# Expert rows of a mixture-of-experts stage: gather and store by bounds, results stored by token

## The chip, the cores and the metric

The kernel runs on one core of a Trainium2 chip. The core has five engines with instruction streams of their own: TensorE (PE; its weight loads are listed apart as PEld), VectorE (DVE), ScalarE (ACT), GpSimd (POOL) and SyncE (SP), which here only issues DMAs. Sixteen DMA engines move data between HBM and the on-chip memory. The metric is the device time of one execution in microseconds; lower is better. Engines wait for each other through semaphores; a DMA raises its semaphore by 16 in all.

## The reference

One layer of a decoder for 1,024 prompt tokens and 64 sample tokens: a forgetting attention and a chunked gating MLP run side by side and are merged, then a mixture of experts, then a gated embedding and the last norm. The change touches the mixture of experts and what reads its result. Everything is float32.

```
def hier_moe(h, w_rg, b_rg, w_re, b_re, w_g, w_u, w_d):     # h: 1088 x 1024
    glog = h @ w_rg + b_rg                                   # 4 groups
    gsel = argmax(glog); pg = softmax(glog)[gsel]
    elog = (h @ w_re + b_re)[group gsel]                     # 8 experts in it
    topv, topi = top_k(softmax(elog), 2); topv /= sum(topv)
    expert_idx = gsel * 8 + topi;  wts = pg * topv
    ...
    yb = (silu(xb @ w_g[e]) * (xb @ w_u[e])) @ w_d[e]        # 1024 -> 512 -> 1024, for each expert's tokens
    out = sum over a token's two experts of wts * yb
...
x2 = x + hier_moe(rmsnorm(x))
x3 = x2 + sigmoid(rmsnorm(x2) @ w_ple_gate + b) * rmsnorm(p @ w_ple_proj)
y  = rmsnorm(x3)
```

So 1,088 tokens make 2,176 rows of expert work, spread over 32 experts. The three weight matrices of an expert are 2 MiB each. With the inputs of the reference the experts get, in order of size, 113, 103, 96, 94, 87, 85, 84, 84, 83, 81, 80, 76, 76, 75, 75, 64, 64, 60, 60, 59, 59, 56, 54, 54, 54, 53, 47, 43, 43, 41, 39 and 34 rows.

## The kernel before, in words

The program is a row of stages, each a block in which all five engines run their own lists; engines meet in a barrier at the end of a block. The last ones are `stage_route` (its engine lists run at the head of the block of `stage_moe`), `stage_moe`, `stage_overflow`, `stage_final`.

**Units.** The rows are laid into 22 units of 128 slots (`NUNIT`), which is 2,816 slots. Experts are ranked by their number of rows. The first 5 fill a unit alone ("full"), from slot 0 up. The next 14 have slots 0 to 95 of a unit, and slots 96 to 127 of two such units together hold one of 7 smaller experts, 32 rows each ("split"). The last 6 share three units, slots 0 to 63 and 64 to 127 ("half"). Within each of these stretches the rows stand at its low end and the empty slots at its high end. Rows over an expert's room would go to up to 25 spare units (`NOVER`), which `stage_overflow` computes in a loop that runs only if there are any; with these inputs there are none.

**Routing.** DVE ranks the experts and computes each row's slot. PE turns this into a list of tokens by slot (`c.bank[2]`, 47 columns of 128 slots, line 2432); an empty slot comes out as token 0. DVE copies the list to `c.idx_i` (lines 2593 and 2594, `c.idx_done`), POOL waits for it, and then DVE works out which expert has which rank (`perm_i`, to line 2602), for which the weight loads from the sixth on wait (`perm_done`).

**The expert loop.** For each unit u: POOL gathers 128 rows of 4 KiB from `moe_in` with one indirect DMA (`gather_rows`, line 2295), PE transposes them (2682), multiplies by gate and up weights (2688), transposes the product (2713) and multiplies by down weights (2727); DVE and ACT keep the intermediate results, ACT copies the unit's result out of PSUM (2763, `keep_y`) and stores it to `moe_out` as a plain block of 128 rows (2765) from its own DMA queue. There are two buffers for gathered rows and two for results. PE's order is fixed: gate(u+1) first half, turn(u), gate(u+1) second half, down(u), transposes(u+2), up(u+1). SP issues the 96 weight loads of 2 MiB in the order in which they are used into a ring of 7 slots (line 2242); each waits until PE is done with what the slot held. Where a unit has four stretches PE runs the four 32-row pieces beside each other.

**The final stage.** For each of 9 tiles of tokens, POOL gathers the two result rows of every token from `moe_out` with two indirect DMAs (2983), by `c.slot_i`; DVE adds them with their weights (3063, 3066); PE, ACT, DVE and POOL do the rest, and SP stores the result. POOL waits first for all stores of results (`c.y_out`).

**Spare rows.** `moe_out` has 47 x 128 rows. While an earlier stage (`stage_mlp` and its neighbours) runs, POOL writes zeros over the 25 x 128 spare rows with five DMAs (line 1083).

Of the kernel before, what the change touches and what calls it, by code (L numbers as in the profile page):

```python
# [21 lines left out]
P = 128  # L22
D = 1024
# [939 lines left out]
def stage_prompt_attention(nc, c):  # L963
# [12 lines left out]
    zeros = view(c, T_AT + 64, D // 2)  # L976
# [10 lines left out]
    blank, c.blank_out = c.sem("blank"), c.kept_sem("blank_out")  # L987
# [26 lines left out]
    with nc.Block() as block:  # L1014
        @block.sync
        def _(sp):
# [47 lines left out]
            sp.wait_ge(c.blank_out, 16 * BLANKS)  # L1064

        @block.gpsimd
        def _(pool):
            pool.wait_ge(c.out_rows, 16 * 5)
            g_ = nc.gpsimd
            g_.memset(zeros, 0.0).then_inc(blank, 1)  # L1070
# [214 lines left out]
BLANKS = 5  # L1285
# [867 lines left out]
SLOTS = (NUNIT + NOVER) * P  # L2153
# [95 lines left out]
def stage_route(nc, c):  # L2249
# [3 lines left out]
    def take(*dims):  # L2253
        v = view(c, at[0], *dims)
        at[0] += int(np.prod(dims))
        return v
# [17 lines left out]
    lane, block_at, tok = take(P), take(NB), take(NT)  # L2274
# [35 lines left out]
    c.idx_i = view(c, T_AT + 3200, NB).bitcast(I32)  # L2310
    c.idx = view(c, T_AT + 40, NB)
    c.over_i = view(c, T_AT + 88, NOVER + 1).bitcast(I32)
    assert NB <= 48 and NOVER < 28
# [33 lines left out]
    def route_pool(pool):  # L2347
# [13 lines left out]
        g.iota(tok, pattern=[[P, NT]], base=0, channel_multiplier=1,  # L2361
# [6 lines left out]
        g.memset(tok[NS:P, NP:NT], 0.0).then_inc(aux, 1)  # L2368
        pool.wait_ge(aux, 10)
        g.memset(PR[NS:P, NPR, :], 0.0).then_inc(aux, 1)  # L2370

# [97 lines left out]
    def route_dve(dve):  # L2469
# [113 lines left out]
        for r in range(2):  # L2583
            tt(ON_BLOCK[:, r], over_tiles(block_at, NB), bcast(hi[:, r], NB), ALU.is_equal)
            tt(ON_BLOCK[:, r], ON_BLOCK[:, r], bcast(tok, NB), ALU.mult)
# [7 lines left out]
        v.tensor_copy(c.idx_i, c.bank[2][:, 0:NB]).then_inc(c.idx_done, 1)  # L2593
        v.tensor_copy(c.idx, c.bank[2][:, 0:NB]).then_inc(c.idx_done, 1)
# [19 lines left out]
def stage_moe(nc, c):  # L2614
# [17 lines left out]
    with nc.Block() as block:  # L2632
# [115 lines left out]
        def _(act):  # L2748
# [9 lines left out]
            def keep_y(u):  # L2758
                b = UNITS[u][0]
# [4 lines left out]
                act.wait_ge(y_done, u + 1)  # L2764
                act.dma_start(c.y_d[b * P:(b + 1) * P, :], Y[:, u % 2, :]).then_inc(y_out[u % 2], 16)
# [44 lines left out]
def stage_overflow(nc, c):  # L2810
# [8 lines left out]
    idx = view(c, T_AT + 116, 1).bitcast(I32)  # L2819
# [13 lines left out]
    with nc.Block() as block:  # L2833
        @block.sync
        def _(sp):
            n = blocks(sp)
            with sp.Fori(0, NOVER // GROUP) as group:
                with sp.If(group * GROUP < n):
                    with sp.Fori(0, GROUP) as j:
                        i = group * GROUP + j  # L2840
                        e = sp.value_load(c.over_i[0:1, bass.ds(i, 1)], min_val=0, max_val=NE - 1)
                        row = i * P + NUNIT * P
# [3 lines left out]
                        sp.wait_ge(y_done, i + 1)  # L2846
                        sp.dma_start(c.y_d[bass.ds(row, P), :], Y).then_inc(stored, 16)
# [4 lines left out]
        def _(pool):  # L2852
            n = blocks(pool)
            with pool.Fori(0, NOVER // GROUP) as group:
                with pool.If(group * GROUP < n):
                    with pool.Fori(0, GROUP) as j:
                        i = group * GROUP + j
                        pool.wait_ge(picked, i + 1)
                        pool.sem_inc(step_end, 1)
                        nc.gpsimd.indirect_dma_start(out=XG, out_offset=None, in_=c.h2_d,  # L2860
                                                     in_offset=bass.IndirectOffsetOnAxis(ap=idx, axis=0)
                                                     ).then_inc(x_in, 16)
# [45 lines left out]
        def _(dve):  # L2908
            v = nc.vector
            n = blocks(dve)  # L2910
            with dve.Fori(0, NOVER // GROUP) as group:
                with dve.If(group * GROUP < n):
                    with dve.Fori(0, GROUP) as j:
                        i = group * GROUP + j
                        v.tensor_scalar(idx, c.idx[:, bass.ds(i + NUNIT, 1)], 1.0, None, ALU.mult).then_inc(picked, 1)
# [8 lines left out]
                                        ALU.mult).then_inc(act_kept, 1)  # L2924

# [7 lines left out]
def stage_final(nc, c):  # L2933
# [22 lines left out]
    with nc.Block() as block:  # L2956
# [194 lines left out]
def finish(nc, c):  # L3151

    with nc.Block() as block:
        @block.sync
        def _(sp):
# [5 lines left out]
            sp.wait_ge(c.blank_out, 16 * BLANKS)  # L3161
# [88 lines left out]
```

## Time and profile before

| what | value |
|---|---|
| median of 3 runs | 1824.93 us (1823.78 to 1824.99) |
| the profiled execution's own time | 1823.42 us |
| its span, first to last instruction | 1821.8 us |
| its mean granted PE clock | 0.969 of full speed |
| expert loop, from the first gate product to the end of the last down product | 1141.27 to about 1660.6 us |
| final stage, first DMA issue to the end of the span | 1668.24 to 1821.8 us |
| bytes read from and written to HBM | 360.50 MB, 52.37 MB |

The profile is of one execution; times are in microseconds from the span's start. In a timeline a row has its start, its length, the engine, the line of the kernel, the operation, what it writes and reads, how many instructions were merged into the row, and in brackets how long the engine had stood idle before it and what ended that. "issue" in brackets is time for which the profile shows no releaser. The DMA share is the mean busy share of the 16 DMA engines.

### The profile page before, as it was taken

The page shows a single profiled execution, that of the slowest core. Times are in us where ns is not written, and L with a number is a line of the kernel's source. Part 1 is how long each engine was busy: PE and PEld are TensorE (multiplying, and loading weights), DVE is VectorE, ACT ScalarE, POOL GpSimd, SP SyncE. Part 2 cuts the span into 40 slices and gives each one's busy share as a digit, 9 for nine tenths or more (in the row PEclk, how much of TensorE's full clock was granted, in tenths as well). Part 3 has the DMA queues.
Part 4 walks back from the last instruction along what each step waited for, and adds up shares of the span by engine and source line. Part 5 has one row for each costly group of instructions (what it writes and reads, how often), then busy time and mean ns, then how long its engine had stood idle before and what let it go on. Part 6 is the DMA issues. An engine that isn't in the chain of part 4 may idle for free. (4 is left out here: it accounts for less than half of the span.)

```text
span 1821.8 us, 27384 instructions
## 1 busy us (share of the span) xinstructions
PE 1692.8 (93%) x10679; PEld 932.2 (51%) x10679; DVE 631.2 (35%) x1233; ACT 309.3 (17%) x565; POOL 291.2 (16%) x375
## 2 busy tenths in 40 slices
PE   7999999998999988988799979999989999995997
PEld 4588888645777753544564435433333334332443
DVE  4622111145555665655134346111001011111565
ACT  2010100012333333321200114100000000000222
POOL 2202212042000021332105410100000000001230
PEclk9999999998999988998899998999999999997999
DMA  6031223202535449998711155999999999998341
GB/s 202 3 86 54 76 68 124 89 0 82 200 107 176 153 146 355 368 383 287 299 48 71 76 221 224 342 404 428 427 426 428 427 427 427 410 426 310 115 150 59
DMA packets 130835, 414.68 MB, mean 228 GB/s; under 512 B 31033, under 2 KB 61306, under 8 KB 118418
## 3 DMA queue, kind: packets, MB, share of 16 engines
q1 hardware_dynamic: 94674, 312.79, 44.8%
q0 software_dynamic: 19488, 68.21, 10.2%
q10 hardware_dynamic: 16544, 31.93, 4.6%
q8 instruction: 86, 1.41, 0.3%
q14 instruction: 43, 0.35, 0.1%
HBM read 360.50 MB, written 52.37 MB: 227 GB/s over the span
## 5 line engine op out<-in xcount | busy, mean ns | idle before, releaser
L2688 PE MATMUL psum<-arena 128*32 128x512 f32 (+2 forms) x2144 | 312.5, 594 | 5.3 <-issue 3.9
L440 PE MATMUL psum<-arena 128*128 128x272 f32 x1120 | 259.5, 393 | 0.0
L440 PEld LDWEIGHTS psum<-arena 128*128 128x128 f32 x1120 | 211.6, 190 | 43.7 <-issue 0.9
L2688 PEld LDWEIGHTS psum<-arena 128*32 128x32 f32 (+2 forms) x2144 | 98.2, 118 | 186.6 <-issue 182.1
L2727 PE MATMUL psum<-arena 128*32 128x512 f32 (+2 forms) x1072 | 159.0, 604 | 13.3 <-issue 11.5
L1146 PE MATMUL psum<-arena 128*128 128x272 f32 x512 | 131.2, 400 | 1.2 <-ACT arena L1174 1.2
L3047 PE MATMUL psum<-arena 128*128 128x512 f32 x256 | 113.7, 602 | 1.4 <-DVE arena L3073 1.4
L2727 PEld LDWEIGHTS psum<-arena 128*32 128x32 f32 (+2 forms) x1072 | 53.4, 120 | 116.1 <-issue 116.1
L2782 DVE TENSOR_TENSOR arena<-psum,g_moe_rows 128x1024 f32<-128x1024 f32 x22 | 26.9, 1224 | 245.8 <-PE psum L2682 245.8
L1974 PE MATMUL psum<-arena 128*128 128x512 f32 x224 | 102.1, 607 | 3.3 <-PEq L1749 1.6
L1146 PEld LDWEIGHTS psum<-arena 128*128 128x128 f32 x512 | 93.6, 193 | 17.0 <-ACT arena L1174 1.3
L2295 POOL DMA_INDIRECT arena<-moe_in,arena x22 | 21.6, 982 | 453.6 <-PE psum L2682 413.2
L3047 PEld LDWEIGHTS psum<-arena 128*128 128x128 f32 x256 | 48.8, 194 | 60.1 <-issue 60.1
L1417 POOL DMA_DIRECT2D arena<-in_cache_v x112 | 60.1, 537 | 117.3 <-PE psum L1521 110.2
L1452 PE MATMUL psum<-arena 128*128 128x512 f32 x160 | 73.4, 601 | 2.6 <-DVE arena L1649 2.6
L1635 DVE STREAM_TRANSPOSE arena<-arena 128x2048 f32<-128x2048 f32 x28 | 63.9, 2297 | 18.7 <-DMA arena<-in_cache_k 18.6
L1974 PEld LDWEIGHTS psum<-arena 128*128 128x128 f32 x224 | 41.7, 193 | 52.3 <-issue 52.3
L2756 ACT ACTIVATE arena<-psum 128x512 f32<-128x512 f32 x22 | 13.1, 597 | 318.6 <-PE psum L2688 318.6
L1181 ACT ACTIVATE arena<-arena 128x128 f32<-128x128 f32 (+7 forms) x64 | 49.1, 768 | 103.6 <-DVE arena L1239 63.2
L2790 DVE TENSOR_TENSOR arena<-arena,psum 128x512 f32<-128x512 f32 x22 | 15.1, 687 | 141.2 <-PE psum L2688 141.2
L887 PE MATMUL psum<-arena 128*128 128x512 f32 x128 | 56.8, 598 | 4.1 <-PEq L132 3.3
L429 PE MATMUL psum<-arena 128*128 128x512 f32 x128 | 56.8, 597 | 0.0
(334 smaller groups left out, 1910.4 us busy)
## 6 DMA issues: line engine op xcount, KB each, us to landing
arena<-in_w_exp_gate SPq DMA_DIRECT2D x32, 2048.0 KB, 17.9
arena<-in_w_exp_up SPq DMA_DIRECT2D x32, 2048.0 KB, 18.5
arena<-in_w_exp_down SPq DMA_DIRECT2D x32, 2048.0 KB, 17.1
arena<-in_cache_v POOLq DMA_DIRECT2D x128, 256.0 KB, 9.3
arena<-in_cache_k SPq DMA_DIRECT2D x124, 256.0 KB, 7.9
arena<-in_w_in SPq DMA_DIRECT2D x18, 1024.0 KB, 6.0
moe_out<-arena POOLq DMA_DIRECT2D x5, 2560.0 KB, 11.1
moe_out<-arena ACTq DMA_DIRECT2D x22, 512.0 KB, 11.4
```

The lines of the kernel that those rows point to most:

```text
L429: last = mm(c.bank[4 + t % 3][:, :], hidden_tile(c, k, t), WV[:, k, :], start=(k == 0), stop=(k == KD - 1))
L440: last = mm(bank[:, s, :], w[:, k, :], x[:, k, SUB * s:SUB * s + SUB], start=start and k == 0, stop=(k == KD // 2 - 1), skip_group_check=True)
L887: last = mm(c.bank[t % 2][:, :], hidden_tile(c, k, t), W[:, k, :], start=(k == 0), stop=(k == KD - 1))
L1146: done = mm(c.bank[7][:, 0:SUB], WG[blk % 2][:, k, q * P:(q + 1) * P], hidden_part(c, k, th, s), start=(k == 0), stop=(k == KD - 1))
L1181: s.activation(S[:, m % 2, hl, 0:w], S[:, m % 2, hl, 0:w], ACT.Exp, bias=low[:, m % 2, hl:hl + 1], scale=-1.0, accum_out=total[:, m % 4, h ...
L1417: pool.dma_start(VC[:, ch, g, :], c.cache_v[bass.ds(numbers[ch][g] * P, P), :]).then_inc(v_in[ch], 16)
L1452: last = mm(c.bank[7][:, :], UP[col % 2][:, n, k, :], src[:, 4 * half:4 * half + 4, k, :], start=(k == 0), stop=(k == KF - 1))
L1635: v.transpose(keys, keys).then_inc(turned[b % 2], 1)
L1974: last = mm(bank, x[:, k, :], w[:, k, :], start=start and k == 0, stop=k == KD // 2 - 1, skip_group_check=True)
L2688: last = mm(out[rows_, :], XT[:, u % 2, k, rows_], c.ring_tile(LOAD[kind, r])[:, k, :], start=(k == 0), stop=(k == KD - 1))
L2727: last = mm(y_ps[rows_, cols], ACT_T[:, k, rows_], c.ring_tile(LOAD["down", r])[:, k, cols], start=(k == 0), stop=(k == KF - 1))
L3047: last = mm(gate_ps[t % 2][:, half * 512:half * 512 + 512], XT[:, t % 2, k, :], c.wpg[half][:, k, :], start=(k == 0), stop=(k == KD - 1))
```

## The change

Empty slots no longer stand for token 0: token numbers are counted from 1, so that an empty slot comes out as 0, and DVE turns the list into two: `c.idx_i`, the row of `moe_in` to gather (first or second expert of the token alike), and `c.dest_i`, the row of `moe_out` to write (the token's number, plus 2,048 for its second expert). Empty slots get an index from 8,191 up in both. Gathers and stores of results are indirect DMAs with `bounds_check` and `oob_is_err=False`, so rows with such an index are left out. The gathered buffer is cleared once on POOL. The stores move from ACT's list to POOL's, as a scatter by token. `moe_out` has 3,136 rows, the first experts' results by token from row 0 and the second experts' from row 2,048, so that the final stage reads plain blocks. The zeros over the spare rows, and the waits for them, are gone. The overflow loop is changed in the same way.

```
-            pool.wait_ge(blank, 1)
-            spare = c.y_d[NUNIT * P:].rearrange("(p n) (a d) -> p (n a) d", p=P, a=2)
-            each = 2 * NOVER // BLANKS
-            for q in range(BLANKS):
-                pool.wait_ge(gate_mm, 5 * q + 4)
-                pool.dma_start(spare[:, q * each:(q + 1) * each, :],
-                               zeros.unsqueeze(1).to_broadcast([P, each, D // 2])).then_inc(c.blank_out, 16)
...
-                             in_offset=bass.IndirectOffsetOnAxis(ap=c.idx_i[:, b:b + 1], axis=0)
-                             ).then_inc(xg_in[u % 2], 16)
+                             in_offset=bass.IndirectOffsetOnAxis(ap=c.idx_i[:, b:b + 1], axis=0),
+                             bounds_check=SEQ + NS - 1, oob_is_err=False).then_inc(xg_in[u % 2], 16)
...
-        g.iota(tok, pattern=[[P, NT]], base=0, channel_multiplier=1,
+        g.iota(tok, pattern=[[SECOND, 2], [P, NT]], base=1, channel_multiplier=1,
...
+        pool.wait_ge(aux, 11)
+        g.memset(XG, 0.0).then_inc(aux, 1)
+        pool.wait_ge(aux, 12)
...
-        v.tensor_copy(c.idx_i, c.bank[2][:, 0:NB]).then_inc(c.idx_done, 1)
-        v.tensor_copy(c.idx, c.bank[2][:, 0:NB]).then_inc(c.idx_done, 1)
+        found = c.bank[2][:, 0:NB]
+        do(v.tensor_scalar(empty, found, 0.5, float(NOWHERE), ALU.is_lt, ALU.mult))
+        do(v.tensor_scalar(other, found, SECOND + 0.5, -float(SECOND), ALU.is_ge, ALU.mult))
+        do(v.scalar_tensor_tensor(out=place_of, in0=found, scalar=-1.0, in1=empty, op0=ALU.add, op1=ALU.add))
+        tt(row_of, place_of, other, ALU.add)
+        v.tensor_copy(c.idx_i, row_of[:, 0:NUNIT]).then_inc(c.idx_done, 1)
+        v.tensor_copy(c.dest_i, place_of[:, 0:NUNIT]).then_inc(c.idx_done, 1)
+        v.tensor_copy(c.idx, row_of[:, NUNIT:]).then_inc(c.idx_done, 1)
+        v.tensor_copy(c.dest, place_of[:, NUNIT:]).then_inc(c.idx_done, 1)
...
-            for u in range(2, NUNIT):
-                pool.wait_ge(xt_tr, u - 1)
-                c.gather_rows(g, u)
+            def gather(u):
+                if u < NUNIT:
+                    pool.wait_ge(xt_tr, u - 1)
+                    c.gather_rows(g, u)
+            def scatter(u):
+                b = UNITS[u][0]
+                pool.wait_ge(y_done, u + 1)
+                g.indirect_dma_start(out=c.y_d, out_offset=bass.IndirectOffsetOnAxis(ap=c.dest_i[:, b:b + 1], axis=0),
+                                     in_=Y[:, u % 2, :], in_offset=None, bounds_check=Y_ROWS - 1, oob_is_err=False
+                                     ).then_inc(y_out[u % 2], 16)
+            gather(2)
+            gather(3)
+            for u in range(NUNIT):
+                scatter(u)
+                gather(u + 4)
...
-                act.wait_ge(y_done, u + 1)
-                act.dma_start(c.y_d[b * P:(b + 1) * P, :], Y[:, u % 2, :]).then_inc(y_out[u % 2], 16)
...
+                n = P if t < NP else NS
                 for r in range(2):
-                    g.indirect_dma_start(out=YG[:, t % 2, r, :], out_offset=None, in_=c.y_d,
-                                         in_offset=bass.IndirectOffsetOnAxis(ap=c.slot_i[:, r, t:t + 1], axis=0)
-                                         ).then_inc(yg_in[t % 2], 16)
+                    at = SECOND * r + t * P
+                    pool.dma_start(YG[0:n, t % 2, r, :], c.y_d[at:at + n, :]).then_inc(yg_in[t % 2], 16)
```

On DVE, at the end of the routing, before the change (2593 and 2594 copy the list for POOL; the two after them begin the ranks for `perm_i`):

```order
L2590 TENSOR_TENSOR arena<-arena 128x384 x6
L2593 CAST arena<-psum 128x47
L2594 COPY arena<-psum 128x47
L2483 TENSOR_TENSOR arena<-arena 1x1024 x2
L2601 TENSOR_REDUCE arena<-arena 1x32
L2602 CAST arena<-arena 1x32
```

and with it:

```order
L2585 TENSOR_TENSOR arena<-arena 128x384 x6
L2589 TENSOR_SCALAR arena<-psum 128x47
L2590 TENSOR_SCALAR arena<-psum 128x47
L2591 SCALAR_TENSOR_TENSOR arena<-psum,arena 128x47
L2478 TENSOR_TENSOR arena<-arena 128x47
L2593 CAST arena<-arena 128x22
L2594 CAST arena<-arena 128x22
L2595 COPY arena<-arena 128x25
L2596 COPY arena<-arena 128x25
L2478 TENSOR_TENSOR arena<-arena 1x1024 x2
L2603 TENSOR_REDUCE arena<-arena 1x32
L2604 CAST arena<-arena 1x32
```

Four operations stand ahead of the first copy, and six instructions more ahead of the ranks.

On POOL, from the routing's last memset to the end of the expert block, before:

```order
L2370 MEMSET arena 64x256
L2295 DMA arena<-moe_in,arena 128x1024 x2
L2378 TENSOR_SCALAR arena<-arena 128x9
L2380 TENSOR_TENSOR arena<-arena,neghalf 128x9
L2295 DMA arena<-moe_in,arena 128x1024 x20
L2632 UNCONDITIONAL_BRANCH
```

and the last of it with the change (2286 is the gather now, 2667 the scatter of results, 2634 the end of the block, 2845 the first read of the overflow block):

```order
L2286 DMA arena<-moe_in,arena 128x1024
L2667 DMA moe_out<-arena 3136x1024
L2286 DMA arena<-moe_in,arena 128x1024
L2667 DMA moe_out<-arena 3136x1024
L2286 DMA arena<-moe_in,arena 128x1024
L2667 DMA moe_out<-arena 3136x1024 x4
L2634 UNCONDITIONAL_BRANCH
L2862 UNCONDITIONAL_BRANCH
L2845 TENSOR_LOAD arena
```

The 22 stores now alternate with the gathers on POOL, and the last four, which wait for ACT's last copies, are the last thing that POOL does in the block.

## Rows read from the trace of the kernel before

**Rows 1.** The page: busy time of each engine, share of the span, instructions.

```profile
PE 1692.8 (93%) x10679; PEld 932.2 (51%) x10679; DVE 631.2 (35%) x1233; ACT 309.3 (17%) x565; POOL 291.2 (16%) x375
```

**Rows 2.** Five stretches: length; busy of PE, PEld, DVE, ACT, POOL; clock, DMA, GB/s.

```profile
1141.27:1276.80 135.53, 135.53 (x840) 51.47 (x840) 15.61 (x18) 9.79 (x12) 8.62 (x9) 1.00 0.96 391
1276.80:1480.00 203.20, 187.81 (x1430) 67.40 (x1432) 20.82 (x24) 13.57 (x17) 7.50 (x8) 0.99 1.01 427
1480.00:1640.00 160.00, 160.00 (x1128) 59.11 (x1124) 18.21 (x21) 11.34 (x14) 4.68 (x5) 1.00 1.00 422
1640.00:1661.00 21.00, 18.04 (x84) 6.17 (x76) 1.38 (x2) 1.35 (x2) 0.00 (x0) 0.92 1.02 407
440.00:620.00 180.00, 179.86 (x1244) 132.31 (x1244) 98.70 (x392) 64.70 (x160) 7.12 (x13) 1.00 0.46 159
```

**Rows 3.** Timeline of PE: start, length, operation, count, [idle before it <-releaser].

```profile
1131.93 7.03 PE L2406 MATMUL psum<-arena 128*128 128x512 f32 x16
1138.80 1.06 PE L2682 MATMUL psum<-ident,arena 128*128 128x128 f32 x8
...
1278.91 7.07 PE L2727 MATMUL psum<-arena 128*32 128x512 f32 x64 [2.11 <-issue]
```

**Rows 4.** The same, later in the expert loop.

```profile
1435.94 1.16 PE L2682 MATMUL psum<-ident,arena 128*128 128x128 f32 x8
...
1458.58 1.16 PE L2682 MATMUL psum<-ident,arena 128*128 128x128 f32 x8
...
1476.32 7.07 PE L2727 MATMUL psum<-arena 128*32 128x512 f32 x64 [1.90 <-issue]
...
1651.85 8.78 PE L2727 MATMUL psum<-arena 128*64 128x512 f32 x32 [1.80 <-DMA arena<-in_w_exp_down]
```

**Rows 5.** DMA from 1340 to 1480 us: queues, then issues with us to landing.

```profile
q1 hardware_dynamic: 3700, 53.94, 90.5%
q0 software_dynamic: 804, 2.90, 5.1%
q10 hardware_dynamic: 785, 2.82, 5.0%
...
moe_out<-arena ACTq DMA_DIRECT2D x5, 512.0 KB, 12.1
arena<-moe_in,arena POOLq DMA_INDIRECT x5, 12.5
```

**Rows 6.** Timeline of DVE: two small chained operations late in the routing.

```profile
1116.46 0.18 DVE L2579 CAST arena<-arena 128x18 int32<-128x18 f32 x1
1116.67 0.18 DVE L2580 TENSOR_SCALAR arena<-arena 128x18 int32<-128x18 int32 x1
```

**Rows 7.** Timeline of POOL: the routing stage's last memset, the first gather.

```profile
1086.55 0.31 POOL L2370 MEMSET arena<- 64x256 f32 x1
1126.78 1.77 POOL L2295 DMA_INDIRECT arena<-moe_in,arena  x1 [39.92 <-DVE arena L2594]
```

**Rows 8.** Timeline of all engines, from the last unit into the final stage.

```profile
1660.67 1.02 ACT L2763 ACTIVATE arena<-psum 128x1024 f32<-128x1024 f32 x1 [18.09 <-PE psum L2727]
1661.72 0.34 ACTq L2765 DMA_DIRECT2D moe_out<-arena  x1
1668.24 0.81 SPq L2961 DMA_DIRECT2D arena<-ple_rows  x2
1669.00 0.94 POOL L2983 DMA_INDIRECT arena<-moe_out,arena  x1 [93.43 <-POOLq L2833]
1670.24 0.94 POOL L2983 DMA_INDIRECT arena<-moe_out,arena  x1 [0.30 <-issue]
...
1676.26 1.28 DVE L3063 SCALAR_TENSOR_TENSOR arena<-arena 128x1024 f32<-128x1024 f32 x1 [25.48 <-DMA arena<-moe_out,arena]
```

**Rows 9.** The page: a group of plain DMAs issued on POOL.

```profile
L1417 POOL DMA_DIRECT2D arena<-in_cache_v x112 | 60.1, 537 | 117.3 <-PE psum L1521 110.2
```

**Rows 10.** DMA issues from 1655 to 1680 us: count, KB each, us to landing.

```profile
moe_out<-arena ACTq DMA_DIRECT2D x1, 512.0 KB, 6.0
```

More of the change, by code:

```diff
@@ L975, in stage_prompt_attention @@
     pace = view(c, T_AT + 24, 16)
-    zeros = view(c, T_AT + 64, D // 2)
     NRAW = 4
@@ L1063, in _ @@
             c.load_keys(sp, 1, 2)
-            sp.wait_ge(c.blank_out, 16 * BLANKS)
         @block.gpsimd
@@ L1069, in _ @@
             g_ = nc.gpsimd
-            g_.memset(zeros, 0.0).then_inc(blank, 1)
             g_.memset(c.CN, 0.0).then_inc(c.cleared, 1)
@@ L1282, in _ @@
                     keep_out(m - 2)
-BLANKS = 5
 CH = 4
@@ L2152 @@
 NOVER = 25
-SLOTS = (NUNIT + NOVER) * P
+SECOND = 2048
+NOWHERE = 8192
+Y_ROWS = SECOND + SEQ + NS
 def unit_plan():
@@ L2273, in stage_route @@
     pick = GT.rearrange("p a b -> p (a b)")[:, 0:NOVER * NE].rearrange("p (s e) -> p s e", e=NE)
-    lane, block_at, tok = take(P), take(NB), take(NT)
+    lane, block_at, tok = take(P), take(NB), take(2, NT)
+    empty, other, place_of, row_of = [take(NB) for _ in range(4)]
     slot_f, lo, hi = take(2, NT), take(2, NT), take(2, NT)
@@ L2309, in stage_route @@
     c.slot_i = view(c, T_AT + 20, 2, NT).bitcast(I32)
-    c.idx_i = view(c, T_AT + 3200, NB).bitcast(I32)
-    c.idx = view(c, T_AT + 40, NB)
+    c.idx_i = view(c, T_AT + 3200, NUNIT).bitcast(I32)
+    c.dest_i = view(c, T_AT + 3200 + NUNIT, NUNIT).bitcast(I32)
+    c.idx, c.dest = view(c, T_AT + 38, NOVER), view(c, T_AT + 38 + NOVER, NOVER)
     c.over_i = view(c, T_AT + 88, NOVER + 1).bitcast(I32)
-    assert NB <= 48 and NOVER < 28
+    assert 2 * NUNIT <= 50 and 2 * NOVER <= 50
     step, aux = c.sem("route_step"), c.sem("route_aux")
@@ L2367, in route_pool @@
         pool.wait_ge(aux, 9)
-        g.memset(tok[NS:P, NP:NT], 0.0).then_inc(aux, 1)
+        g.memset(tok[NS:P, :, NP:NT], 0.0).then_inc(aux, 1)
         pool.wait_ge(aux, 10)
         g.memset(PR[NS:P, NPR, :], 0.0).then_inc(aux, 1)
+        pool.wait_ge(aux, 11)
+        g.memset(XG, 0.0).then_inc(aux, 1)
+        pool.wait_ge(aux, 12)
         pool.wait_ge(c.idx_done, 2)
@@ L2584, in route_dve @@
             tt(ON_BLOCK[:, r], over_tiles(block_at, NB), bcast(hi[:, r], NB), ALU.is_equal)
-            tt(ON_BLOCK[:, r], ON_BLOCK[:, r], bcast(tok, NB), ALU.mult)
+            tt(ON_BLOCK[:, r], ON_BLOCK[:, r], bcast(tok[:, r], NB), ALU.mult)
         for ch in range(NCHUNK):
@@ L2758, in keep_y @@
             def keep_y(u):
-                b = UNITS[u][0]
                 act.wait_ge(down_mm, u + 1)
@@ L2818, in stage_overflow @@
     ACT_T, Y = view(c, MOE_AT + 5 * D, KF, P), view(c, MOE_AT + 6 * D, D)
-    idx = view(c, T_AT + 116, 1).bitcast(I32)
+    idx, dest = view(c, T_AT + 116, 1).bitcast(I32), view(c, T_AT + 117, 1).bitcast(I32)
     gate_ps, up_ps, turn_ps, y_ps, x_ps = c.bank[0], c.bank[1], c.bank[2], c.psum_pair(2), c.psum_pair(3)
@@ L2841, in _ @@
                         e = sp.value_load(c.over_i[0:1, bass.ds(i, 1)], min_val=0, max_val=NE - 1)
-                        row = i * P + NUNIT * P
                         for w, src, n_rows in ((wg, c.w_gate, D), (wu, c.w_up, D), (wd, c.w_down, FF)):
@@ L2845, in _ @@
                                          ).then_inc(w_in, 16)
-                        sp.wait_ge(y_done, i + 1)
-                        sp.dma_start(c.y_d[bass.ds(row, P), :], Y).then_inc(stored, 16)
                         sp.wait_ge(stored, i * 16 + 16)
@@ L2857, in _ @@
                         i = group * GROUP + j
-                        pool.wait_ge(picked, i + 1)
+                        pool.wait_ge(picked, i * 2 + 2)
                         pool.sem_inc(step_end, 1)
                         nc.gpsimd.indirect_dma_start(out=XG, out_offset=None, in_=c.h2_d,
-                                                     in_offset=bass.IndirectOffsetOnAxis(ap=idx, axis=0)
-                                                     ).then_inc(x_in, 16)
+                                                     in_offset=bass.IndirectOffsetOnAxis(ap=idx, axis=0),
+                                                     bounds_check=SEQ + NS - 1, oob_is_err=False).then_inc(x_in, 16)
+                        pool.wait_ge(y_done, i + 1)
+                        pool.sem_inc(step_end, 1)
+                        nc.gpsimd.indirect_dma_start(out=c.y_d, out_offset=bass.IndirectOffsetOnAxis(ap=dest, axis=0),
+                                                     in_=Y, in_offset=None, bounds_check=Y_ROWS - 1, oob_is_err=False
+                                                     ).then_inc(stored, 16)
         @block.tensor
@@ L2914, in _ @@
                         i = group * GROUP + j
-                        v.tensor_scalar(idx, c.idx[:, bass.ds(i + NUNIT, 1)], 1.0, None, ALU.mult).then_inc(picked, 1)
+                        v.tensor_scalar(idx, c.idx[:, bass.ds(i, 1)], 1.0, None, ALU.mult).then_inc(picked, 1)
+                        v.tensor_scalar(dest, c.dest[:, bass.ds(i, 1)], 1.0, None, ALU.mult).then_inc(picked, 1)
                         dve.wait_ge(x_tr, i + 1)
@@ L2924, in _ @@
                                         ALU.mult).then_inc(act_kept, 1)
+                        dve.wait_ge(stored, i * 16 + 16)
 def final_weights(c):
@@ L3160, in _ @@
             sp.wait_ge(c.consts_in, 16 * 7)
-            sp.wait_ge(c.blank_out, 16 * BLANKS)
             for sem in c.h2_out:
@@ L3245 @@
     c.e_d = nc.dram_tensor("ple_rows", (SEQ + NS, D), F32).ap()
-    c.y_d = nc.dram_tensor("moe_out", (SLOTS, D), F32).ap()
+    c.y_d = nc.dram_tensor("moe_out", (Y_ROWS, D), F32).ap()
     program(nc, c)
```

1 line of the change is left out of this document (removed).

## The prediction, made before the changed kernel ran

> **What bounds the kernel now.** The page's busy line comes first: TensorE is busy for 1692.8 of 1821.8 us [rows 1], so other engines matter only where PE waits or where the DMA engines are full. A table by stretches then splits the part that the change touches [rows 2]. From 1141 to 1277 us PE does not pause and the DMA share climbs to 0.96. From 1276.8 to 1480 the DMA engines are at 1.01 with 427 GB/s and PE is busy for 187.81 of 203.20: it stands still for 15.39 us. From 1480 to 1640 it does not pause. PE's timeline shows what the idle time looks like: pauses of 2 to 3 us ahead of a product, the first of 2.11 us at 1276.8 and the last of 1.90 us before 1476.32 [rows 3, 4]. The profile names no releaser ("issue"), but each stands ahead of a product whose weights must have landed, inside a stretch with full DMA engines; the one before 1651.85 (1.80 us) is named, a down weight [rows 4]. I read them all as late weights. A unit without a pause takes PE 22.64 us (1435.94 to 1458.58 [rows 4]).
>
> So the loop is within a few per cent of two limits. The weights are 32 x 3 x 2.097 = 201 MB; gathers and stores add 22 x 2 x 0.524 = 23 MB. In the full stretch the weights have 90.5% of the engines' time, POOL's queue with the gathers 5.1%, ACT's queue with the stores 5.0% [rows 5]. Behind the loop, the timeline shows the last result copied at 1661.69, stored from ACT at 1661.72, the next block entered at 1668.24 and the first final gather at 1669.00 [rows 8]. From 1677 on PE runs the final stage nearly alone.
>
> **The change part by part.**
>
> *Zeros over spare rows.* They ran between 455 and 620 us. There PE is busy for 179.86 of 180 us and the DMA engines are at 0.46 [rows 2]. Nobody waited; removing them gives at most the 0.14 us. I take 0.
>
> *Routing.* DVE has four more operations ahead of the first copy. Chained operations of this size start 0.21 us apart (1116.46, 1116.67 [rows 6]): 0.84 us, so the first gather goes from 1126.78 [rows 7] to 1127.6. PE is in the embedding's products until it takes up the gathered rows at 1138.80 without a pause [rows 3]; if the gather lands as the store at a quiet moment did, in 6.0 us [rows 10], it is there at 1133.6, 5 us early; with the 12.5 us of the full loop [rows 5] at 1140.1, which would cost at most the 0.84 that it starts later. The ranks, and the sixth weight load behind them, come 0.84 + 2 x 0.12 = 1.1 us later. The loads after it wait for slots that PE frees, so the delay is not carried on. I take 0, bounds 0 and +1.1. Clearing the gather buffer on POOL is 128x2048 against 64x256 in 0.31 us [rows 7]: at most 2.5 us, in 40 us in which POOL waits [rows 7]. Cost 0.
>
> *Empty slots.* 2,816 - 2,176 = 640 slots are empty, 22.7%. Each gather and each store shrinks by 0.119 MB on average, 0.28 us at 427 GB/s. What this is worth is decided by how the bytes are spread over the 16 DMA engines. A weight has landed only when all 16 have added their part (the code waits for multiples of 16). If the saving is spread evenly, all are ahead by 0.28 us per transfer. If each engine serves fixed slots it is not: the empty slots stand at the high end of their stretches. With the counts of the reference's inputs slots 0 to 42 are full in every unit, slots 0 to 58 in all but the three shared by halves; 596 of the 640 empties lie in slots 59 to 127. Engines that serve the low slots then move what they moved before, and PE waits for them. No row shows which engine serves a slot; the bounds come from PE's pauses. Below: nothing saved, 0. Above: nine units lie between the first and the last pause of the full stretch, 9 x 2 x 0.28 = 5.0 us of traffic, plus the first pause of 2.11, which what was saved earlier covers: 7.1 us; and the 1.80 before 1651.85: 8.9 in all. The row nearest to the question is the full stretch at 1.01: no engine has spare time to give to another, so a saving counts only on the engine that has it. The empties lie on the high slots, so I take the lower end, 0, for this part.
>
> The Trainium skill ("DMA: Bandwidth & Descriptors", The descriptor swizzle) gives such a fixed assignment for a 128-partition transfer from GpSimd: eight engines serve partitions 0 to 63, eight 64 to 127, in groups of four. By it the engine with partitions 0 to 3 and 32 to 35 would have no empty slot in any unit, and the sum stays at 0; whether an indirect transfer with left-out rows follows it no row here shows.
>
> *One queue fewer.* Stores and gathers were in flight together, 12.1 and 12.5 us each [rows 5], on two queues beside the weights. On POOL's one queue they go one behind the other, and both have 45 us (two units) until needed, so part of this traffic moves behind weights that PE waits for. In a backlog such a shift counts once, not per unit: at most one transfer, 0.524 MB at 427 GB/s = 1.2 us. I take -1.2, bounds -1.2 and 0. On POOL the scatter waits for ACT's copy, and behind it is queued the gather for four units on; it comes about 1 us later and is needed 45 us later. ACT loses 0.34 us per unit [rows 8], in idle time.
>
> *End of the block.* The last store was 0.34 us on ACT after the copy; as an indirect DMA it is 0.94 us on POOL (the final gathers' length [rows 8]) plus about 0.1 us for the wait. POOL reaches the barrier at 1661.69 + 1.04 = 1662.7 instead of ACT at 1662.06: +0.7. The store's landing took 6.0 us [rows 10], to 1667.7, before the first final gather at 1669.00; a scatter that starts moving 0.7 us later lands at 1668.4, and the gather is then due at 1669.7. Covered by 1.3 us. I take +0.7, bounds +0.4 and +5.3 (below, C).
>
> *Final reads.* The first two gathers are issued 1.24 us apart [rows 8]. A plain DMA on POOL takes 0.54 us [rows 9], with the same 0.3 between: 0.84. The second read is 0.4 us earlier; part is lost since the rows come at the engines' rate. I take -0.3, bounds -0.8 and +0.5. The later ones lie beside PE.
>
> Sum: 0 + 0 + 0 - 1.2 + 0.7 - 0.3 = -0.8 us. The profiled execution took 1823.42 us, 1.6 over its span and 1.5 under the median of 1824.93; with the change it would take 1822.6, and the median comes to 1824.1. By the bounds without C and without an even saving, -2.0 to +2.3: 1822.5 to 1827. About 0.2% (3.7 us) is what a measurement of this kernel can tell from no change; "same" is 1821.3 to 1828.6.
>
> **The rivals.**
>
> *A, the forecast:* the engines with the low slots keep their traffic. 1824.1.
>
> *B, the saving is even over the engines* (left-out rows are packed away before rows are dealt out, or slots are dealt out in turn). For it: 22.7% less in both kinds of transfer, and PE's 15.39 us of pauses under a DMA share of 1.01. Against it: the empties' place. Up to -8.9 with the tail's +0.4: 1816.4; dealt out in turn (slot modulo 16) the engine with the fewest empties has 26 where the mean is 40, two thirds of it, so -5.9 + 0.4: 1819.4. Chance 27%.
>
> *C, the last scatter lands late.* The slower side. In the loop a gather from POOL takes 12.5 us to land beside the weights [rows 5], and the last scatter meets the 4 MB of final-stage weights that SP issued just before. The final reads wait for it. If it takes 12.5 us from 1661.8, they start at 1674.3 instead of 1669.0, +5.3, and nothing is behind which to hide it; it decides from a landing of 7.9 us on. Against it: the plain store there landed in 6.0 [rows 10]. 1824.9 + 5.3 - 1.2 - 0.3 = 1828.7, more where the scatter's rows, spread over HBM, take longer. Chance 12%.
>
> The Trainium skill ("DMA: Bandwidth & Descriptors", Latency and other measured facts) gives the first byte as about 1 us for DMAs from GpSimd and 0.6 for those from SP and ACT; by it the last landing would be 0.4 later, inside the cover.
>
> *D, the change doesn't do what it says:* a left-out row costs its engine as much as a moved one. The loop keeps its time apart from the queue: also 1824.1, or with nothing from the queue 1825.3. Chance 8%.
>
> **How the numbers follow.** A 53%, B 27%, C 12%, D 8%. Likeliest: 1824.1, its own range 1822.5 to 1827. B lies below 1821.3 with nearly all of its weight, and A with a little: faster 28%. C, at 1828.7 or more, gives slower with two thirds of its weight, and the unknown costs in A and D add 4%: 12%. Same 60%. The range from 1817.0 to 1828.4 leaves out half of C and the far half of B.
>
> **What would show it.** Right: in the changed profile PE's idle time in the stretch from 1277 to 1480 is still 12 us or more, while the bytes of POOL's queue in the loop are about 23% under those of the two queues before; the first final read starts 0.5 to 1 us later after ACT's last copy; PE's work up to 1141 is at the same times within 1 us. Wrong: the pauses shrink to half or less (B); the final reads are released by the scatter's landing (C); POOL's queue moves as many bytes as the two before (D).

## The result and the profile after the change

The changed kernel took 1825.82 us (median of 20 runs, 1818.86 to 1830.17) where the kernel before took 1822.78 us beside it (20 runs, 1818.99 to 1827.71). The ratio is 1.0017, 95% interval 1.0010 to 1.0025: 3 us slower. The forecast was 1824.1 against 1824.93, no change that can be measured. The time lies inside its range; the side is that of rival C, and what was forecast for the parts is far from what was measured, as shown below.

The page's busy line of the changed kernel, its windows (columns as in [rows 2]):

```profile
PE 1695.7 (93%) x10679; PEld 933.2 (51%) x10679; DVE 631.2 (35%) x1239; ACT 309.3 (17%) x565; POOL 304.0 (17%) x392
```

```profile
1141.27:1276.80 135.53, 135.20 (x840) 51.20 (x838) 15.63 (x18) 9.72 (x13) 13.98 (x13) 1.00 0.96 392
1276.80:1480.00 203.20, 191.85 (x1452) 69.53 (x1456) 20.83 (x24) 13.32 (x17) 16.23 (x16) 0.98 1.00 423
1480.00:1640.00 160.00, 160.00 (x1126) 58.92 (x1119) 18.23 (x21) 12.24 (x15) 12.16 (x12) 1.00 0.99 413
...
440.00:620.00 180.00, 179.86 (x1243) 132.63 (x1243) 98.80 (x392) 65.44 (x162) 2.27 (x8) 1.00 0.28 89
```

The zeros over spare rows are gone (159 to 89 GB/s in the last row) and PE is busy for the same 179.86 us. In the full stretch PE stands still for 11.35 us where it was 15.39 [rows 2].

The DMA queues from 1160 to 1640 us, first of the kernel before (packets, MB, share), then of the changed one:

```profile
DMA packets 17903, 201.02 MB, mean 419 GB/s; under 512 B 1983, under 2 KB 1983, under 8 KB 6847
...
q10 hardware_dynamic: 2880, 10.49, 5.4%
q0 software_dynamic: 2592, 9.44, 4.8%
```

```profile
DMA packets 18015, 198.28 MB, mean 413 GB/s; under 512 B 3062, under 2 KB 3062, under 8 KB 6860
...
q0 software_dynamic: 5472, 15.56, 8.1%
```

POOL's one queue moves 22% less than the two did (15.56 against 19.93 MB). The packets under 512 B rose by 1079, and the 4.37 MB that are missing are 1067 rows of 4096 bytes: in the records a left-out row is a packet of 4 bytes and 9 ns where a moved row has 4096 bytes and 159 ns.

The timeline of the changed kernel from the last unit into the final stage, to be held against [rows 8]:

```profile
1655.71 1.02 ACT L2779 ACTIVATE arena<-psum 128x1024 f32<-128x1024 f32 x1 [15.57 <-PE psum L2744]
1657.51 0.98 POOL L2667 DMA_INDIRECT moe_out<-arena  x1 [15.62 <-ACT arena L2779]
1670.58 0.82 SPq L2979 DMA_DIRECT2D arena<-ple_rows  x2
1671.12 2.19 POOL L3003 DMA_DIRECT2D arena<-moe_out  x4 [12.64 <-POOLq L2847]
1677.90 1.28 DVE L3081 SCALAR_TENSOR_TENSOR arena<-arena 128x1024 f32<-128x1024 f32 x1 [29.57 <-DMA arena<-moe_out]
```

The last copy starts 4.96 us earlier than before and the first final read 2.12 us later. The span is 1.9 us longer, and this divides into four pieces, between the first gate product, the last copy, the first read and the first sum on DVE:

| piece | after, us | before, us | difference |
|---|---|---|---|
| start of the loop | 1140.93 | 1141.27 | -0.34 |
| loop | 514.78 | 519.40 | -4.62 |
| copy to first read | 15.41 | 8.33 | +7.08 |
| read to sum | 6.78 | 7.26 | -0.48 |

Together they are +1.64; the rest comes later.

What stands in the 15.41 us is seen only when one asks for the line that ends the block (events of the engines' sequencers: count, ns, start). The changed kernel:

```profile
L2634 POOLq EVENT_SEMAPHORE  x2: 17/17/17, 1665.1 to 1665.2; - x2
L2634 DVEq DRAIN  x1: 725/725/725, 1647.7 to 1647.7; - x1
L2634 SPq DRAIN  x1: 123/123/123, 1647.8 to 1647.8; - x1
...
L2634 ACTq DRAIN  x1: 1052/1052/1052, 1655.7 to 1655.7; - x1
L2634 POOLq DRAIN  x1: 7469/7469/7469, 1657.3 to 1657.3; - x1
```

And the kernel before, the same line of it:

```profile
L2632 POOLq EVENT_SEMAPHORE  x2: 17/17/17, 1662.3 to 1662.4; - x2
L2632 POOLq DRAIN  x1: 14061/14061/14061, 1574.4 to 1574.4; - x1
...
L2632 SPq DRAIN  x1: 123/123/123, 1651.8 to 1651.8; - x1
...
L2632 ACTq DRAIN  x1: 157/157/157, 1662.1 to 1662.1; - x1
```

At a block's end each engine drains, then all meet. In the kernel before SP and ACT drain in 0.12 and 0.16 us although their DMAs are in flight: ACT had issued a store 0.4 us before, which landed at 1667.7. ACT's 1.05 us in the changed kernel lie beside its last copy; no DMA of its own is in flight then. POOL's drain is another thing: 7.47 us here, 14.06 us before, where it began behind the last gather and lay beside the loop. Before, the last gather landed at 1587.5 and the drain ended at 1588.5. In the changed kernel the last scatter was issued at 1657.51 and took 5.4 us to land, to 1662.9; the drain ends at 1664.8, 1.9 us later, and the engines meet at 1665.2. Before they met at 1662.4, 0.7 us after the copy's end; now it is 8.5 us. Behind it the overflow block takes its 5.2 us (1665.3 to 1670.5; before 5.8, 1662.4 to 1668.2), which used to cover the store's landing and now stands in series with it. There POOL's drain, with nothing of its own in flight, takes 0.05 to 0.06 us in both kernels, so the 7.47 us are not what a drain on POOL always costs. The row of 14.06 us was there to be read before.

### The profile page after: what moved, and what is told of

It is laid out like the page before. It is cut to its first block and busy times, and to the rows that moved or that the text cites. A ratio compares the mean times of both kernels' runs of the same rounds, so it can differ in the third digit from the quotient of the medians.

```text
span 1823.7 us, 27423 instructions
## 1 busy us (share of the span) xinstructions
PE 1695.7 (93%) x10679; PEld 933.2 (51%) x10679; DVE 631.2 (35%) x1239; ACT 309.3 (17%) x565; POOL 304.0 (17%) x392
## 5 line engine op out<-in xcount | busy, mean ns | idle before, releaser
L2667 POOL DMA_INDIRECT moe_out<-arena x22 | 22.2, 1008 | 461.7 <-PE psum L2699 280.2
```

## The experiments

Each ratio is to the kernel before, run beside it. "Loop" is, here and below, the time from the start of the loop's first gate product to the start of its last copy, in the profiled execution. The start itself moves between 1138 and 1147 us from one profile to another, so spans alone compare badly. Two profiles of one and the same kernel gave loops of 515.14 and 516.51, of another 518.96 and 518.94. The loop of the kernel before was 519.40, and 517.59 in the run below that changes its last store alone. A difference between two loops of under 2 us is therefore not read as one.

**Is it POOL's drain?** The first kernel is the changed one with the last unit's scatter issued from the overflow block:

```
-            for u in range(NUNIT):          # expert block, POOL
+            for u in range(NUNIT - 1):
...
+            nc.gpsimd.indirect_dma_start(out=c.y_d, ...)   # overflow block, POOL, first
```

> The changed kernel, with the last unit's scatter issued at the head of the overflow block instead of at the end of the expert block. Drain theory (at the end of a block POOL's drain waits until its last DMA has landed; in the changed kernel it lasts 7.47 us and holds all engines at the barrier): POOL's drain in the expert block is short, the landing hides behind the 5 us of the overflow block's own instructions, and the first final read comes 4.5 to 6 us sooner after the last copy than in the changed kernel, so the time is 0.9970 to 0.9990 of the kernel before. Rival (the scatter's issue and landing are themselves what the final stage waits for): the same delay only moves into the next block; ratio 1.001 to 1.003.

1819.72 us, ratio 0.9978 (0.9968 to 0.9988). Its timeline and its drains:

```profile
1657.19 1.02 ACT L2779 ACTIVATE arena<-psum 128x1024 f32<-128x1024 f32 x1 [15.58 <-PE psum L2744]
1659.53 0.97 POOL L2864 DMA_INDIRECT moe_out<-arena  x1 [16.17 <-issue]
1665.10 0.82 SPq L2983 DMA_DIRECT2D arena<-ple_rows  x2
1665.63 2.19 POOL L3007 DMA_DIRECT2D arena<-moe_out  x4 [5.12 <-POOLq L2847]
```

```profile
L2634 POOLq EVENT_SEMAPHORE  x2: 17/17/17, 1658.3 to 1658.4; - x2
L2634 POOLq DRAIN  x1: 10172/10172/10172, 1642.2 to 1642.2; - x1
...
L2634 ACTq DRAIN  x1: 1052/1052/1052, 1657.2 to 1657.2; - x1
```

The drain of the expert block is not short, as expected, but 10.17 us, and hidden beside the last unit; the scatter's landing lies beside the overflow block. From copy to first read it is 8.44 us, against 8.33 before the change. Against the changed kernel the ratio falls by 0.39%, 7.1 us: as much as the +7.08.

The landing is not hidden in full. In the overflow block POOL drains again, now with the scatter in flight:

```profile
L2847 POOLq DRAIN  x1: 2662/2662/2662, 1662.2 to 1662.2; - x1
L2847 PEldq DRAIN  x1: 13/13/13, 1663.6 to 1663.6; - x1
```

The scatter landed at 1664.76 and this drain ended at 1664.85, 1.3 us after PE, the last of the others, was ready.

The other way round, the kernel before with its last plain store moved from ACT to POOL, with the waits for it, and nothing else:

```
+            pool.wait_ge(y_done, NUNIT)
+            pool.dma_start(c.y_d[b * P:(b + 1) * P, :], Y[:, (NUNIT - 1) % 2, :]).then_inc(c.y_last, 16)
...
+                if u == NUNIT - 1:              # ACT: no store of the last unit
+                    return
```

> The kernel before, with the last unit's store alone, still a plain block of 128 rows, issued from POOL instead of ACT. Drain theory: POOL's drain lasts until the store has landed, 5 to 8 us, and the first final read comes 4 to 8 us later after the last copy: ratio 1.002 to 1.0045. Rival (it is the indirect form or the scattered rows that cost): under 1 us, ratio 1.000 to 1.0005.

1830.35 us, ratio 1.0036 (1.0024 to 1.0049).

```profile
1663.04 1.02 ACT L2767 ACTIVATE arena<-psum 128x1024 f32<-128x1024 f32 x1 [16.30 <-PE psum L2731]
1664.36 0.59 POOL L2662 DMA_DIRECT2D moe_out<-arena  x1 [84.64 <-ACT arena L2767]
1677.24 0.81 SPq L2967 DMA_DIRECT2D arena<-ple_rows  x2
```

```profile
L2633 POOLq DRAIN  x1: 7448/7448/7448, 1664.3 to 1664.3; - x1
```

The store landed at 1670.79, the drain ended at 1671.78, and the first read came 14.98 us after the copy, 6.65 later than before. So the cost needs neither the indirect form nor left-out rows: one 512 KB store issued from POOL as the last thing of a block costs 7.4 us of drain and makes this kernel 0.36% slower.

**Are the left-out rows worth something in the loop?** The changed kernel with nothing left out (an empty slot gathers row 0 and is stored to a spare row of its own), and the kernel before with bounds on its gathers alone, stores plain on ACT:

> The changed kernel with nothing left out: empty slots gather row 0 again and are stored to spare rows of their own, so that the bytes are those of before and only the queue (gathers and scatters both on POOL) is new. If the queue shortened the pauses: PE idle in 1277 to 1480 stays near 11 us and the ratio is near that of the changed kernel, 1.001 to 1.0025. If the bytes did it: PE idle back at 15 us, ratio 1.003 to 1.005, since the drain stays.

> The kernel before, with only the gathers leaving out empty slots (and the list prepared for it); stores stay plain blocks on ACT. Theory that the bytes left out shorten PE's pauses: half of the bytes, so about half of the 4 us by which the pauses between 1277 and 1480 us shrank, no longer block end: ratio 0.9980 to 0.9995. Rival (one DMA queue fewer is what shortened the pauses): pauses as before, 15 us, ratio 0.9995 to 1.0005.

Full rows: 1830.14 us, 1.0031 (1.0018 to 1.0045), loop 518.98. Short gathers on the kernel before: 1820.87 us, 0.9986 (0.9975 to 0.9998), loop 516.22. By the loops 4.2 us hang on the rows of the changed kernel (518.98 against 514.78) and 3.2 on the gathers' of the kernel before (519.40 against 516.22), by the ratios 2.6 in both pairs, where the forecast had 0. The next three test its reason, the fixed slots: they are the kernel with the late scatter, and their gathers leave out more slots of every unit, full ones too. The edit is a column `far` with 8192 on the named slots, added to the gathers' rows:

```
+        do(v.memset(far, 0.0))
+        do(v.memset(far[64:128], 8192.0))
...
         tt(row_of, place_of, other, ALU.add)
+        tt(row_of, row_of, far, ALU.add)
```

> The kernel with the late last scatter, in which the 22 gathers leave out slots 64 to 127 as well (835 more rows, 3.42 MB; the rows computed for them are stale, scatters as before). 1819.72 us and 13.61 us of pauses between 1276.8 and 1480 are the base. Theory A (each DMA engine serves fixed slots, four by four, eight engines the low 64 and eight the high 64): the engines with the fullest slots still move 176 rows each, nothing is saved, pauses stay at 12 to 15 us and the time at 1819.7 within 1.5. Theory B (what is left is spread evenly): nine units of the stretch save 1.40 MB, 3.3 us at 427 GB/s: pauses near 10, time near 1816. By A eight of the sixteen parts of a gather's landing come several us ahead of the others, by B all come together.

> As the kernel without the high 64 slots, but the gathers leave out slots 32 to 63 and 96 to 127 (1068 more rows than the late last scatter, 4.37 MB). Theory A: every one of the sixteen engines has half of its slots left out, the fullest goes from 176 rows to 88: over nine units 2.36 MB at the whole rate, 5.5 us; pauses near 8, time near 1814. Theory B: 4.37 of 22 units are 1.79 MB in nine, 4.2 us; pauses near 9.5, time near 1815.5. So by A this kernel is 4 to 6 us faster than the one without the high 64 slots, by B within 1 us of it.

> As the two others, but the gathers leave out slots 0 to 63 (1341 more rows, 5.49 MB). Theory A: the eight engines of the high slots still move up to 146 rows where the fullest engine moved 176, 17% less: at most 1.9 us over nine units; pauses near 12, time 1818 to 1819.5. Theory B: 2.25 MB in nine units, 5.3 us; pauses near 8.5, time near 1814.5.

Without the high 64: 1821.43 us, 0.9987 (0.9975 to 0.9998), loop 517.26. Without the low 64: 1819.24 us, 0.9982 (0.9973 to 0.9991), loop 516.29. Without 32 to 63 and 96 to 127: 1812.85 us, 0.9944 (0.9931 to 0.9956), loop 509.41. The windows of the full stretch, of the late scatter and then of the three in that order:

```profile
1276.80:1480.00 203.20, 189.59 (x1444) 69.27 (x1440) 20.82 (x24) 13.56 (x17) 16.20 (x16) 0.99 1.01 423
```

```profile
1276.80:1480.00 203.20, 190.90 (x1429) 68.68 (x1425) 20.84 (x24) 13.56 (x17) 16.20 (x16) 0.98 1.00 416
```

```profile
1276.80:1480.00 203.20, 188.76 (x1436) 68.76 (x1432) 20.84 (x24) 13.57 (x17) 16.19 (x16) 0.99 0.99 412
```

```profile
1276.80:1480.00 203.20, 195.73 (x1496) 69.77 (x1492) 22.06 (x25) 14.60 (x18) 17.04 (x17) 0.98 1.01 424
```

The low 64 are the most rows (1341 against 1068) and gain nothing; the spread ones gain 0.34% and take PE's idle time from 13.61 to 7.47 us. Bytes saved on one set of eight engines are worth nothing, on both sets they are worth about what they weigh. An even spread (B) is refuted: it expected 3.3 and 5.3 us from the high and the low 64.

**But then why do the empties count?** They leave the engines of the lowest slots what they had. Four kernels look at this: full rows with the late scatter, so without the drain's cost, then the same with a row of its own for each empty slot instead of row 0, then that with the high and with the low half of the gathers left out:

> The kernel with the late last scatter, with every slot gathered and stored (empty ones read row 0 and go to spare rows of their own). It isolates what the left-out rows are worth, free of GpSimd's drain at the end of the block. 640 rows in each direction, 5.24 MB; nine units of the full stretch have 2.14 MB of it, 5.0 us. Theory A (fixed slots): the same as with the rows left out, 1819.7 within 1.5. Theory B (even): 4 to 9 us slower, 1824 to 1828. A third (the changed kernel against the one with full rows gave 1825.8 against 1830.1): about 4 us of the loop hang on the rows, 1824, with loop times from the first gate product to the last copy of 519 us instead of 515.

> The kernel with the late last scatter and full rows (1824.5 us, loop 518.96 us from the first gate product to the last copy), but an empty slot gathers a row of its own (8 x its slot + its unit modulo 8) where 640 empty slots read row 0, as in the kernel before. Theory H (the 4 us that the left-out rows gain in the loop are the price of reading one row hundreds of times): loop near 515, time near 1820. Theory S (the engines of the high slots are a little behind in any case, so that their 596 empty rows count until they are level with the others) and theory B (bytes count evenly): nothing changes, loop 519, 1824.5.

> As the kernel with own rows for the empties, but the gathers leave out slots 64 to 127 (1408 rows, 5.77 MB; the rows computed for them are stale). Stores are full. Theory S: the engines of the high slots are relieved until the low ones bound: 4 us less than with own rows, loop 515, 1820. Theory H: nothing against own rows. Theory B: 5.77 of 23 MB, 5.5 us over nine units: loop 513.

> As the one before, but the gathers leave out slots 0 to 63. Theory S: the engines of the high slots bound and keep all they had: the same as with own rows, loop 519, 1824.5. Theory H: the same too, but at the level of own rows of 515. Theory B: loop 513, as with the high slots left out.

Full rows 1824.52 us, 1.0010 (0.9998 to 1.0022), loop 518.96. Own rows 1823.71 us, 0.9997 (0.9985 to 1.0009), loop 519.24: reading one row for all empties is not the price. Without the high half 1826.01 us, 1.0014 (1.0005 to 1.0022), loop 519.42; without the low half 1825.68 us, 1.0014 (1.0005 to 1.0023), loop 522.98 (why its loop is longer is not known; its time isn't). So it isn't the high engines alone that hold the loop either, nor the low ones alone. One direction at a time, between new runs of both ends:

> Late last scatter, empty slots left out of the gathers alone; the stores carry them to spare rows of their own. If the gathers bring the 4 us: loop 515, 3 to 5 us faster than full rows. If the stores do (all kernels with short stores had 515 to 517, all with full ones 519 to 523): loop 519, as with full rows. If the sum of bytes counts: half way, 517.

> Late last scatter, empty slots left out of the stores alone; the gathers read row 0 for them. If the stores bring the 4 us: loop 515 and the time of the late last scatter, 3 to 5 us faster than full rows. If the gathers: loop 519. If bytes: 517.

> The kernel with the late last scatter once more, as the lower end beside the two others: loop 515 within 1.5 if its length repeats, ratio 0.998 to the kernel before.

> The late last scatter with full rows once more, as the upper end: loop 519 within 1.5, ratio 1.000 to 1.002. If this and the late last scatter come within 1.5 us of each other, the 4 us were spread from run to run.

Both left out 1820.11 us, 0.9982 (0.9969 to 0.9994), loop 516.51. Gathers alone 1819.99 us, 0.9987 (0.9975 to 0.9998), loop 515.53. Stores alone 1820.69 us, 0.9991 (0.9976 to 1.0007), loop 516.80. Neither 1825.51 us, 1.0015 (1.0003 to 1.0028), loop 518.94. Either one brings nearly all of it. A gain that is used up after the first half fits single engines which lag and catch up; that is a reading, which the landings below bear on.

Part of what separates the medians lies behind the loop. From copy to first read it is 7.20 us with both left out and 9.67 with neither: in the overflow block POOL's drain waits for a scatter that is shorter in the one (1.42 us of drain) and longer in the other (3.89).

The landing events show how level the engines are. A weight's landing has sixteen parts, one for each DMA engine. Below they are sorted, in us before the last one, median over the 27 or 28 weights that landed from 1300 to 1480 us:

```
full rows, again     -3.8 -3.6 -3.5 -3.5 -3.4 -2.8 -2.6 -2.3 -2.2 -1.8 -0.8 -0.7 -0.5 -0.3 -0.2  0
gathers cut          -8.4 -7.2 -6.6 -4.1 -4.0 -3.3 -3.3 -2.9 -2.9 -2.7 -2.4 -2.4 -2.2 -1.4 -1.3  0
both cut, again     -10.0 -8.9 -8.1 -5.7 -4.5 -3.8 -2.9 -2.8 -2.7 -2.6 -2.5 -2.5 -2.2 -1.9 -1.7  0
without 64-127       -9.4 -9.1 -8.4 -8.3 -8.3 -8.1 -7.9 -7.7 -2.1 -2.0 -1.7 -1.4 -1.1 -0.6 -0.4  0
and 16-31, 48-63     -9.1 -9.0 -8.9 -8.4 -8.3 -8.2 -7.8 -7.7 -7.6 -7.5 -7.3 -7.2 -1.1 -0.6 -0.3  0
and 0-15, 32-47      -9.4 -9.4 -9.4 -9.2 -8.9 -8.9 -8.4 -8.4 -8.2 -8.2 -7.8 -7.3 -1.8 -0.7 -0.2  0
and 28-31, 60-63     -9.3 -9.0 -8.9 -8.6 -8.4 -8.4 -8.1 -7.9 -7.4 -2.2 -2.0 -1.5 -1.1 -0.9 -0.4  0
```

With full rows six parts, the last among them, land within 0.8 us. With the empties cut in one or both directions a single part comes 1.3 to 1.7 us behind all others, which fits engines with empties that came last and, once relieved, don't any more. The events don't say which engine a part belongs to.

The last three rows are these kernels, each the one without the high half and with a further part of the low slots left out of the gathers:

> Stores full, empties with rows of their own, gathers without slots 64 to 127 (loop 519.4 us, 1826.0) and without 16 to 31 and 48 to 63, which by theory A belong to the last four of the eight low engines. Theory L (one of these four lags some 3 us behind the engines with slots 0 to 15 and 32 to 47; it had 12 to 20 of 176 rows empty, 1.9 to 3.2 us at 159 ns): loop 515 to 517, time 1821 to 1824. Without a laggard there: 519.5 as before.

> The same with slots 0 to 15 and 32 to 47 left out instead. Theory L: the laggard keeps its rows, 519.5 us, 1825 to 1826. If the engine that holds the loop is one of the first four: 515 to 517, and then the fixed slots don't explain the gain of the left-out empties, as the first engines had none or up to nine.

> The same with slots 28 to 31 and 60 to 63 alone left out of the low ones: by theory A one engine, the low one with the most empties (20). If it is the laggard: loop 515 to 517 as with all four; if another of the four is: 519.5.

Eight parts run ahead without the 64 high slots, then exactly twelve, twelve and nine: eight slots, 28 to 31 and 60 to 63, are one engine's. That is the fixed assignment which the prediction weighed, and the swizzle of the Trainium skill ("DMA: Bandwidth & Descriptors", The descriptor swizzle) holds here for indirect gathers with left-out rows too. In time: without 16 to 31 and 48 to 63 1822.99 us, 0.9995 (0.9984 to 1.0005), loop 516.99, so 2.4 us come back, 3.5 by the ratios, whose intervals just touch; without 0 to 15 and 32 to 47 1826.18 us, 1.0013 (1.0004 to 1.0022), loop 520.13, nothing. What holds the low half is thus among the four engines that had 12 to 20 empties (1.9 to 3.2 us in each direction at 159 ns), one of them or several, and relieving the two without any empty row gains nothing. The engine with 20 alone: 1824.96 us, 1.0002 (0.9993 to 1.0012), loop 519.79. The time leans to it by 0.12%, inside the intervals, the loop doesn't; which of the four it is stays open. No run splits the high half in this way.

The Trainium skill ("DMA: Bandwidth & Descriptors", Latency and other measured facts) says that engines 7 and 15 are usually slower than the others in traces. By its swizzle engine 7 serves 28 to 31 and 60 to 63, and engine 15 the slots with the most empties. The pair of halves that both have to be relieved agrees; the run on engine 7 alone doesn't settle it. I had not weighed this rule.

## Why the prediction was wrong

- **End of the block**, forecast +0.7, bounds +0.4 and +5.3: this step failed. It had POOL reach the barrier once the scatter was issued, at 1662.7, and the landing covered by the overflow block with 1.3 us to spare. But POOL's drain lasts until its DMAs have landed, and the overflow block comes behind that. Copy to first read +7.08 us, beyond the upper bound too, confirmed both ways (7.1 us back with the scatter moved; 0.36% lost with a plain store moved to POOL). The other terms together were forecast at -1.5 and came to -5.4 (start, loop and final reads). That the time still lies inside the range is luck: misses of +6.4 and -3.9 us nearly cancel.
- **Rival C** had the side, not the mechanism: the scatter landed in 5.4 us, under its 7.9, and the final reads were released by the barrier. The landing did count, but through the drain, ahead of the overflow block, where no cover is left.
- **Empty slots**, forecast 0: the fixed slots are right and B is refuted, yet "the engines with the low slots keep their traffic" was taken for "the loop keeps its time". The second doesn't follow from the first, because engines that had empties came last as well: 3.4 us with the gathers' empties left out (518.94 to 515.53), 2.1 with the stores', 2.4 to 4.2 with both. The sign that I had named for A, 12 us or more of idle PE, came out at 11.35, in between. It can't decide: the same loop showed 13.61 us with the late scatter, and that of the kernel before 13.46 in the run that moved its last store.
- **One queue fewer**, forecast -1.2: full rows on one queue gave loops of 518.94 to 519.24 and ratios of 0.9997 to 1.0015, two queues loops of 519.40 and 517.59. No gain from it can be seen.
- **Rival D** is refuted: 9 ns for 159, and a gain where full rows have none.
- **Final reads**, forecast -0.3: -0.48. **Routing**: the first gather was issued at 1128.84, 2.06 us later instead of 0.84, and PE took up its rows at 1138.47 without a pause, as costed. **Zeros**: 0, as forecast.
- **The range**: the bounds of the single terms give -1.6 at the lower end, not the -2.0 of the prediction, and 1822.5 lies lower still. The result lies at the other end, so nothing hangs on it.

Sum by the measured terms: -0.3 (start), -4.6 (loop), +7.1, -0.5, and some 0.3 behind: +1.9 us in the span, +3 in the medians. The kernel with the late scatter keeps the loop's gain without the drain and beats both: 1819.72 and 1820.11 us, ratios 0.9978 and 0.9982.

## What to carry to other kernels

Before an instruction is moved to another engine, read that engine's drain at the end of the block, on the line that closes it, even where it is hidden: one that is 14 us long beside a loop is 7 us on the path once the last DMA is issued late. Keep the last DMA ahead of a barrier off POOL, or issue it behind the barrier, where the next block is long enough to cover its landing. Bytes saved in a full DMA stretch count on the engines that come last: sort the sixteen parts of a landing to see how level they are, and spread what is left out over all engines. Here 1341 rows left out on eight engines gained nothing, 1068 spread over sixteen 0.34%.

## What the runs showed of the hardware

- POOL's drain at the end of the expert block took 7.45 to 14.06 us with its own DMAs in flight, plain or indirect, and ended 0.9 to 1.9 us after the last of them had landed (the kernel before, the changed one, the two with the last store or scatter moved). In the overflow block it took 2.66 us with the late scatter in flight and 0.05 to 0.06 with nothing. In the kernel before SP's took 0.12 and ACT's 0.16 us with theirs in flight.
- A row left out by bounds is a packet of 4 bytes, 9 ns; 4096 bytes take 159 ns.
- A gather's slots belong to fixed engines: without the slots of 8, 12, 12 and 9 of them exactly so many parts of a weight's landing came 7 to 9 us ahead.
- Eight engines with no gathered rows run 8 to 9 us ahead in a full stretch and change the loop by nothing (519.24 to 519.42).
